# An encoder layer with 16 experts on one core: the experts' in-projection split by gate and value instead of by column half

## The reference, cut to what matters

```python
for e in range(N_EXPERTS):
    a, u = jnp.split(t @ w_ei[e], 2, axis=-1)
    y = y + gate[:, e:e + 1] * ((jax.nn.silu(a) * u) @ w_eo[e]).astype(F32)
```

## Time and profile before

| | |
|---|---|
| median of 3 runs | 1547.08 us (1546.88 to 1547.58) |
| the profiled execution: its own time | 1546.55 us |
| the profiled execution: span of the records | 1544.8 us |
| PE busy | 1332.0 us (86%) |
| DVE busy | 759.1 us (49%) |
| ACT busy | 621.3 us (40%) |
| DMA, mean over the span | 144 GB/s |

### The profile page before, as it was taken

The page is one execution under the profiler, slowest core; times in us unless marked ns, Lnnn a source line. Parts: engine busy times, 40 slices in busy tenths (PEclk is TensorE's granted clock), DMA queues, the critical chain, the costliest instruction groups (busy, mean ns, idle before and its releaser), DMA issues.

```text
span 1544.8 us, 21064 instructions
## 1 busy us (share of the span) xinstructions
PE 1332.0 (86%) x7598; PEld 1129.0 (73%) x7599; DVE 759.1 (49%) x1000; ACT 621.3 (40%) x709; POOL 334.0 (22%) x319
## 2 busy tenths in 40 slices
PE   3999999999997899999999997138899999899940
PEld 1889878888796788977888897136688778778830
DVE  2332355321642432355421463618865766875548
ACT  2332444332313322254422222327755664874521
POOL 1232000000302043000000112443523532653214
PEclk9999999999995799999999997559999999999975
DMA  7944400034462344310024431749977977997233
GB/s 165 261 90 101 91 1 1 1 82 137 109 164 111 83 92 100 83 28 1 1 59 128 114 83 74 258 135 302 350 256 230 320 240 256 323 345 249 78 118 142
DMA packets 161418, 222.49 MB, mean 144 GB/s; under 512 B 20775, under 2 KB 136103, under 8 KB 160535
## 3 DMA queue, kind: packets, MB, share of 16 engines
q1 hardware_dynamic: 137296, 177.40, 39.5%
q0 software_dynamic: 12800, 34.74, 8.1%
q10 hardware_dynamic: 11244, 9.29, 1.9%
HBM read 200.14 MB, written 34.35 MB: 152 GB/s over the span
## 4 chain that ended last, share of the span: by engine, by line
issue 56%; PE 19%; POOL 8%; DMA 7%; DVE 5%; ACT 2%; ACTq 2%; SPq 0%; POOLq 0%; DVEq 0%
PE banks L645 5%; PE banks L647 5%; PE banks L646 5%; DMA moe_raw<-in_w_expert_in 2%; POOL gated L534 1%; POOL pt L510 1%; DMA moe_raw<-in_w_expert_out 1%; POOL prob L517 1%; POOL slots L550 1%; ACTq L1000 1%; PE banks L871 1%; DMA toeplitz_rows<-bias_rows 1%; DVE moe_lo L1552 1%; PE banks L893 1%; ACT moe_hi L1163 1%
## 5 line engine op out<-in xcount | busy, mean ns | idle before, releaser
L1552 DVE TENSOR_TENSOR moe_lo<-moe_raw,moe_hi 128x2048 fp32r<-128x2048 f32 x102 | 233.1, 2289 | 75.6 <-ACT moe_hi L1163 75.5
L1163 ACT ACTIVATE moe_hi<-moe_raw 128x2048 fp32r<-128x2048 f32 x102 | 195.0, 1915 | 65.1 <-PE banks L647 37.4
L1269 DVE TENSOR_TENSOR wlo<-raw,whi 128x2048 fp32r<-128x2048 f32 (+1 forms) x56 | 125.2, 2236 | 182.7 <-ACT whi L1022 182.7
L645 PE MATMUL banks<-wlo,xT 128*128 128x256 f32 x640 | 183.5, 287 | 7.7 <-DVE xT L1379 4.5
L646 PE MATMUL banks<-whi,xT 128*128 128x256 f32 x640 | 182.6, 285 | 0.0
L647 PE MATMUL banks<-whi,xT 128*128 128x256 f32 x640 | 182.5, 285 | 0.0
L645 PE MATMUL banks<-xT,whi 128*128 128x512 f32 x448 | 174.7, 390 | 0.0
L646 PE MATMUL banks<-xT,whi 128*128 128x512 f32 x448 | 174.4, 389 | 0.0
L647 PE MATMUL banks<-xT,wlo 128*128 128x512 f32 x448 | 174.3, 389 | 0.0
L1022 ACT ACTIVATE whi<-raw 128x2048 fp32r<-128x2048 f32 (+1 forms) x56 | 103.5, 1849 | 120.8 <-PE banks L647 120.8
L645 PE MATMUL banks<-moe_lo,xeh 128*128 128x512 f32 x368 | 147.1, 400 | 5.7 <-DVE xel L1558 4.3
(11 more groups left out here) (222 smaller groups left out, 2330.5 us busy)
## 6 DMA issues: line engine op xcount, KB each, us to landing
moe_raw<-in_w_expert_in SPq DMA_DIRECT2D x128, 512.0 KB
raw<-in_w_in SPq DMA_DIRECT2D x80, 512.0 KB, 6.4
moe_raw<-in_w_expert_out SPq DMA_DIRECT2D x64, 512.0 KB
raw<-in_w_out SPq DMA_DIRECT2D x16, 512.0 KB, 5.5
toeplitz_rows<-bias_rows POOLq DMA_DIRECT2D x4, 1152.0 KB, 12.7
kqv<-in_x SPq DMA_DIRECT2D x8, 512.0 KB, 9.4
pt<-in_x SPq DMA_DIRECT2D x2, 2048.0 KB, 9.1
raw<-in_w_branch_a SPq DMA_DIRECT2D x8, 512.0 KB, 6.2
```

The source lines that it names most:

```text
L645: mm(dst, left[0], right[1], start=first, stop=False)
L1163: A(moe_hi[m % SPLIT_E], moe_raw[m % RAW_E], ACT.Copy).then_inc(e_hi, 1)
L1269: V.tensor_tensor(view(wlo[c % 2], shape), view(raw[c % 2], shape), view(whi[c % 2], shape).bitcast(F32), ALU.subtract).then_inc(w_split, 1)
L1552: V.tensor_tensor(moe_lo[m % SPLIT_E], moe_raw[m % RAW_E], moe_hi[m % SPLIT_E].bitcast(F32), ALU.subtract).then_inc(e_lo, 1)
```

## The change

The same numbers are computed by as many products. What moves:

- Chunks 0 and 1 hold all 512 gate columns (for the two halves of the input features), chunks 2 and 3 all 512 value columns. A load is still 512 KB, two for a chunk, but it covers two blocks of input features with all 512 columns: pieces of 2 KB.
- Gates now stand in banks 2 and 3, values in banks 0 and 1. ACT takes the silu of all gates in one operation of 128 x 1024 straight into `h_full`, behind chunk 1. DVE multiplies in place, in two operations that both stand behind the last chunk.
- TensorE transposes the next step's rows (first part) and then both halves of the product behind the last chunk, one after the other. The out-projection's first part is no longer interrupted.
- All four copies of the results to `y_sb` are made by ACT; DVE has none, and the semaphore `y_dve` is gone.

```diff
-                        ei = w_ei[0, bass.ds(e, 1)].rearrange("o (k p) (a m n) -> p (o k) a m n", p=P, a=2, m=HALVES)
+                        ei = w_ei[0, bass.ds(e, 1)].rearrange("o (k p) (a n) -> p (o k) a n", p=P, a=2)
...
-                                for a in range(2):
-                                    sp.dma_start(v[:, :, a], ei[:, ks, a, c // 2]).then_inc(e_raw[n % RAW_E], 16)
+                                for k in (0, 2):
+                                    sp.dma_start(v[:, k:k + 2], ei[:, k0 + k:k0 + k + 2, c // 2]).then_inc(e_raw[n % RAW_E], 16)
...
 TensorE
-                    if kh == 0:
-                        pe.wait_ge(h_done, z * HALVES + half + 1)
+                    if c == 2:
+                        pe.wait_ge(h_done, z * HALVES + 2)
...
-                    if c == 2:
-                        turn_acts(0)
-                        rows_of_next(0)
+                pe.wait_ge(silu_done, z + 1)
+                rows_of_next(0)
+                turn_acts(0)
+                turn_acts(1)
...
-                out_part(0, 0, (0,))
-                turn_acts(1)
-                last = out_part(0, 0, (1,))
+                last = out_part(0, 0)
+                if width > P:
+                    pe.wait_ge(h_lo, z * HALVES + 2)
+                    last = out_part(0, 1)
+                last.then_inc(e_used, 1)
+                rows_of_next(1)
...
 ACT
+                        def gates():
+                            act.wait_ge(e_used, SPLIT_E + z * ECH + 2)
+                            act.wait_ge(h_turned, z * HALVES + 2)
+                            A(h_full.rearrange("p (r n) -> p r n", r=2), two[1].rearrange("p (r n) -> p r n", r=2), ACT.Silu) \
+                                .then_inc(silu_done, 1)
...
-                        for d in range(2):
-                            A(y_sb[b][:, d * 512:(d + 1) * 512], bank[4 + d][:, :], ACT.Copy, scale=slot_gate(b, 0)).then_inc(y_act, 1)
+                        for c in range(2):
+                            for d in range(2):
+                                A(y_sb[b][:, c * D + d * 512:c * D + (d + 1) * 512], bank[4 + 2 * c + d][:, :], ACT.Copy,
+                                  scale=slot_gate(b, c)).then_inc(y_act, 1)
...
 DVE
+                            if half == 0:
+                                dve.wait_ge(e_used, SPLIT_E + z * ECH + XCH)
+                                dve.wait_ge(silu_done, z + 1)
+                            h = h_full.rearrange("p (r n) -> p r n", r=2)[:, :, half * HW:(half + 1) * HW]
+                            V.tensor_tensor(h, h, two[0].rearrange("p (r n) -> p r n", r=2)[:, :, half * HW:(half + 1) * HW],
```

More of the change, by code:

```diff
@@ L289, in encoder_kernel @@
         xe = [[place(f"xe{n}{i}", KD * SLOTS, F32R) for n in ("h", "l")] for i in range(2)]
-        silu = place("silu", 2 * SLOTS)
-        h_full = place("h_full", 2 * SLOTS)
+        h_full = place("h_full", 2 * DE)
         hT = [place(f"hT{i}", 4 * SLOTS, F32R) for i in range(2)]
@@ L913, in turn_acts @@
                     if half == 0:
-                        pe.wait_ge(y_act, z * 2 + 1)
-                        pe.wait_ge(y_dve, z * 2 + 1)
+                        pe.wait_ge(y_act, z * 4 + 1)
                     for q in range(2):
                         for r in range(width // P):
-                            last = nc.tensor.transpose(tb[:, q * SLOTS + r * P:q * SLOTS + (r + 1) * P],
-                                                       h_full[:, r * HW + q * P:r * HW + (q + 1) * P], ident)
+                            o = r * DE + half * HW + q * P
+                            last = nc.tensor.transpose(tb[:, q * SLOTS + r * P:q * SLOTS + (r + 1) * P], h_full[:, o:o + P], ident)
                     last.then_inc(h_turned, 1)
@@ L932, in step @@
                         for k in range(KD // 2):
-                            last = mm3(bank[2 - 2 * half + r][:, :], [v[:, kh * (KD // 2) + k, r * P:(r + 1) * P] for v in xv],
+                            last = mm3(bank[2 - 2 * value + r][:, :], [v[:, kh * (KD // 2) + k, r * P:(r + 1) * P] for v in xv],
                                        [v[:, k] for v in w], kh == 0 and k == 0, kh == 1 and k == KD // 2 - 1)
                     last.then_inc(e_used, 1)
-                    if c == 2:
-                        turn_acts(0)
-                        rows_of_next(0)
+                pe.wait_ge(silu_done, z + 1)
+                rows_of_next(0)
+                turn_acts(0)
+                turn_acts(1)
                 def out_part(c, r, halves=(0, 1)):
@@ L1180, in _ @@
                         z = pair * 2 + b
-                        def gated_half(half):
-                            act.wait_ge(e_used, SPLIT_E + z * ECH + 2 * half + 2)
-                            A(silu.rearrange("p (r n) -> p r n", r=2),
-                              two[1 - half].rearrange("p (r a n) -> p r a n", r=2, a=2)[:, :, 0], ACT.Silu).then_inc(silu_done, 1)
+                        def gates():
[3 more added lines that the diff above has]
+                                .then_inc(silu_done, 1)
                         def acts_hi(half):
@@ L1446, in _ @@
             used = 16
-            for sm, k in ((e_used, SPLIT_E), (e_lo, RAW_E), (rows_T, 8), (xe_lo, 2), (h_done, 2), (h_turned, 2), (y_act, 1), (y_dve, 1)):
+            for sm, k in ((e_used, SPLIT_E), (e_lo, RAW_E), (rows_T, 8), (xe_lo, 2), (h_done, 2), (h_turned, 2), (y_act, 1)):
                 for _i in range(k):
@@ L1571, in gated_half @@
                         def gated_half(half):
-                            dve.wait_ge(h_turned, z * HALVES + half + 2)
-                            dve.wait_ge(silu_done, z * HALVES + half + 1)
-                            V.tensor_tensor(h_full.rearrange("p (r n) -> p r n", r=2), silu.rearrange("p (r n) -> p r n", r=2),
-                                            two[1 - half].rearrange("p (r a n) -> p r a n", r=2, a=2)[:, :, 1],
+                            if half == 0:
[3 more added lines that the diff above has]
+                            V.tensor_tensor(h, h, two[0].rearrange("p (r n) -> p r n", r=2)[:, :, half * HW:(half + 1) * HW],
                                             ALU.mult).then_inc(h_done, 1)
@@ L1583, in _ @@
                         e_split(pair, b * ECH + SPLIT_E)
+                        e_split(pair, b * ECH + 1 + SPLIT_E)
                         gated_half(0)
-                        e_split(pair, b * ECH + 1 + SPLIT_E)
+                        gated_half(1)
                         acts_lo(0)
+                        acts_lo(1)
                         rows_lo(1 - b, z + 1, 0)
                         e_split(pair, b * ECH + 2 + SPLIT_E)
-                        gated_half(1)
-                        acts_lo(1)
+                        rows_lo(1 - b, z + 1, 1)
                         e_split(pair, b * ECH + 3 + SPLIT_E)
-                        rows_lo(1 - b, z + 1, 1)
                         e_split(pair, b * ECH + 4 + SPLIT_E)
-                        dve.wait_ge(e_used, SPLIT_E + z * ECH + ECH)
-                        dve.wait_ge(y_gone, z + 1)
-                        dve.wait_ge(scatter_ids_in[b], pair * 16 + 16)
-                        for d in range(2):
-                            V.tensor_scalar(y_sb[b][:, D + d * 512:D + (d + 1) * 512], bank[6 + d][:, :], slot_gate(b, 1), None,
-                                            ALU.mult).then_inc(y_dve, 1)
                         e_split(pair, b * ECH + XCH + 1 + SPLIT_E)
```

24 lines of the change are left out of this document (9 added, 15 removed).

## The result

| | before | after |
|---|---|---|
| median of the runs on one chip | 1546.98 us (4 runs, 1543.78 to 1547.58) | 1565.9 us (4 runs, 1556.11 to 1569.77) |
| the profiled execution: its own time, span | 1546.55, 1544.8 us | 1562.95, 1561.3 us |

The changed kernel is slower: its time is 1.0122 of the time before, 95% interval 1.0081 to 1.0163. The forecast was 1550.6 us with a range up to 1558.0, so the direction was right and the size was not: some 19 us instead of 3.5.

The account below looks back on a forecast made before the run. Wide steps were taken as bound by TensorE, narrow ones by TensorE, DVE, ACT and DMA close together, with order deciding. 6.9 - 6.4 + 2.0 + 1.0 = +3.5 us gave 1550.6 us, range 1543.5 to 1558.

Parts of the forecast that it names:

- Wide steps, +6.9 us: Seven wide steps in the experts: uncovered waits behind the last in-projection product make each 0.99 us longer, +6.9 us together.
- T: In a step of the experts, the end of the slot of the last in-projection product; the out-projection was forecast T+3.02 in wide steps.
- The walk of a narrow step: Narrow steps in the experts, by ACT's and DVE's queues: 21.87 us with b = 0, 20.47 with b = 1; -6.4 us altogether.
- a narrow step: products start 0.228 apart: TensorE in narrow steps: 48 in-projection products and a restart take 11.04 us, within a step of 20.37 plus DVE's delay.
- DMA, +2.0 us: Loads in steps 1, 2, 3, 11 and 12: 0.4 us each as the queue can run dry, bounds 0 and 6.
- the gap: In-projection loads: 6.3 us without a new load between the low parts of positions 1 and 2; a chunk lasts 3.3.
- The end, +1.0 us: Behind the last step: ACT alone makes the result copies in 2.43 us where the slower pair took 1.41, +1.0 us.
- Rival 3: Pieces gain nothing, loads come late, six narrow steps each 1.5 us longer: +14, 1561 us; chance 0.14.
- ACT's waits for transfers: Sign: waits of ACT's splits for loads in steps 1 to 3 and 10 to 12, to decide on rivals about late loads.
- Rival 2: Faster: narrow steps all come down to 20.37 us as DMA and DVE work lighten, -6.2, 1540.9; chance 0.16 including half way, 1544.

## Why the prediction was wrong, by its own steps

- **Wide steps, +6.9 us: right.** 36.83 to 36.86 us each, +7.3 for seven. The split of the idle time differs a little (0.3 and 0.88 us where 0.1, 0.3 and 1.0 were named), the out-projection starts 3.17 behind T where 3.02 was worked out, and cutting by row blocks gave the microsecond back.
- **The walk of a narrow step: right as a walk.** DVE starts at 12.70 (12.74), the double silu holds ACT for 0.90 us (1203.32 to 1204.22; 0.91), and steps without a fall take 21.76 to 21.84 with b = 0 (21.87) and 20.76 and 20.91 in steps 3 and 11 (20.47). One saving was read too high: step 8 took 23.02 us before, not the 23.32 of step 6, so it had 1.15 to give and not 1.45.
- **The failed step: "a narrow step: products start 0.228 apart", for all products, in a step whose waits I had just put together.** The walk adds a wait at its own length and keeps every product at the 2.4 GHz level; the granted clock was read as a constant of these steps since the earlier trace rows showed 1.00 in all four stretches, and no term, no rival and no end of the range let it move. With the waits of 1.25 and 1.36 us half a step apart the clock had held; with 1.59 and 0.75 next to each other it fell. That cost 24.5 - 21.87 = 2.6 us in each of steps 6, 8 and 10 and 1.6 in step 2. Step 12 is also 2.65 us over its walk, of which 1.1 is the longer wait (2.70 for 1.59) and some 1.6 the clock; step 1 is 2.05 over, of which about 0.4 is a longer wait, as in steps 3 and 11. So the clock took about 12.6 us (7.8 + 1.6 + 1.6 + 1.6), which agrees with TensorE's busy time, up by 13.2, against a miss of 12.45 in the narrow steps. The late loads' 1.5 us belong to the +2.0 below, and step 0 came out 0.9 us shorter.
- **DMA, +2.0 us: its parts right.** The rate of 2 KB pieces was 377 to 380 GB/s (373), the gap is there, and steps 3 and 11 are 0.3 and 0.4 us over the walk: ACT's split of position 2 starts late, in step 11 after 2.20 us of waiting for its load, and the copies of `hT` stand behind it. With step 12's 1.1 and step 1's 0.4 that makes 2.2 us. That 2 KB earn anything in the end is shown by neither comparison (1.0122 against 1.0114, 0.9953 against 0.9969). The rate was not capped at the figure that the prediction quotes from the Trainium skill, "DMA: Bandwidth & Descriptors", section "Where 436 GB/s comes from": 2 KB pieces brought 381 and 391 GB/s.
- **The end, +1.0 us: right.** 62.43 for 61.43.
- **Rival 3, the queue that runs dry, had a time near the result (1561) by another mechanism.** The prediction named the rows that decide: ACT's waits for transfers. They fell, from 14.1 us over the experts before to 12.0 (6.8 to 5.0 in steps 1 to 3, but up from 1.7 to 5.7 in 10 to 12), and cost TensorE about 2 us by the sum above, an estimate, not the 14 of the rival. In the stretch at 0.50 of step 6 the DMA share is 1.03, and filling TensorE alone took 2.7 us out of the step. Where the clock was held, though, these waits grew to 22.0 and, with all narrow steps filled, 22.7 us, and TensorE waited for late loads in steps 2, 6, 8 and 12. Rival 2 named the right point, the four copies and the table load ahead of the second split; what passing it costs was taken as 1.5 us of delay and is, with the clock, some 4.1.

What was seen and not drawn on: the sums of idle time hardly differ between the kernels (25.1 and 27.2 us), so a ledger of waits can't find this loss. The row that does is busy time at equal counts beside the clock.

The Trainium skill, "TensorE: Matmul & The Clock Gate", section "HAM oscillation — how this bites in real kernels", describes kernels whose clock goes back and forth between its two levels since TensorE waits between groups of products, and advises an order that keeps it busy. The trace agrees on the alternation (30.7 us at 0.50 in the experts), and products put into the waits kept the clock at 1.00 in steps 6, 8 and 10. A fifth rival, "the waits meet and the clock falls", was missing from the prediction.

**What stays open.** Nearly equal waits brought the clock down in one step and not in another (step 6 fell in the changed kernel at 1.59 and 0.75 us, and took 21.84 at 1.00 with 1 KB pieces at 1.60 and 0.88; single waits of 2.48 us brought it down in two of three steps; and in the kernel before single waits of 1.49 and 1.56 did not, where 1.35 did in step 1 of the changed kernel). So that the waits stand together is not shown to be what matters; that filling them keeps the clock up is. The runs scatter with the clock: the changed kernel took 1556.11 us at a mean clock of 0.932 and 1568.86 at 0.923, and the kernel before 1538.19 at 0.938 and 1549.16 at 0.931. What decides in the single case no run here told.

## What to carry to other kernels

Before merging two waits of a busy TensorE into one place, price not only their length but the stretch behind them at half clock: here 2.3 us of waits cost 2.6 more, and in another kernel, where later waits could shrink, only 0.3. Read busy time at an equal count of instructions next to the granted clock; if it grew, the loss is not in the list of waits, and a handful of products that nobody reads, put into the wait, tests it in one run; here it took back 8.5 of 19 us, and with the result copies shared all of it. Then look again at the loads: a faster TensorE asks for them earlier. And cut a product between two phases by what is complete first (row blocks) rather than by columns that all complete last.

## What the runs showed of the hardware that I had not expected

- Two waits of 1.59 and 0.75 us with four transposes between them, in a step otherwise filled with products, were enough for the granted clock to fall to 0.50; over the six falls of this run it stayed there for 3.4 or 6.8 us and came back while TensorE was busy. The fall does not come each time: with waits of 1.60 and 0.88 us it held at 1.00.
- At 0.50 a product of 512 columns starts every 0.43 us instead of every 0.23, so 6.8 us there cost 2.7 (24.48 - 21.76) and 3.4 us cost 1.6 (22.26 - 20.68).
- Six products in the longer wait did as much as nine in both (1.0069 against 1.0071), though the clock still fell in two of the filled steps, behind what was left of the waits.
- A load in 2 KB pieces reached 377 to 380 GB/s at a full share, against 322 in 1 KB, and the kernel's time did not show it.
